# The causal mask of the forget-gate heads: subtracted from the decay by VectorE instead of multiplied in by TensorE

## The reference

```
def causal_block_attention(q, k, v, scale, log_decay=None):
    ...
        s = jnp.einsum('bhqd,bhkd->bhqk', qi, k, preferred_element_type=jnp.float32) * scale
        if log_decay is not None:
            s = s + args[2][..., :, None] - log_decay.astype(jnp.float32)[:, :, None, :]
        q_pos = i * Q_BLOCK + jnp.arange(Q_BLOCK)
        mask = key_pos[None, :] <= q_pos[:, None]
        s = jnp.where(mask, s, jnp.finfo(jnp.float32).min)
        p = jax.nn.softmax(s, axis=-1)
        return jnp.einsum('bhqk,bhkd->bhqd', p.astype(v.dtype), v)
    ...
    log_f = jax.nn.log_sigmoid(f_logit.astype(jnp.float32) + b_forget.astype(jnp.float32))
    c = jnp.cumsum(log_f, axis=1).transpose(0, 2, 1)
    o_fox = causal_block_attention(heads(fq), heads(fk), heads(fv), FOX_HEAD_DIM ** -0.5, c)
```

## Time and profile before

| | us |
|---|---|
| median of three runs (lowest, highest) | 2709.56 (2707.67, 2709.72) |
| span of the profiled execution, first to last instruction | 2705.4 |
| attention loop, 352.2 to 659.6 | 307.4 |
| first forget-gate half, 388.0 to 427.3 | 39.3 |
| first latent half after it, 427.3 to 464.5 | 37.2 |

### The profile page before, as it was taken

The page is one execution under the profiler, slowest core; times in us unless marked ns, Lnnn a source line. Parts: engine busy times, 40 slices in busy tenths (PEclk is TensorE's granted clock), DMA queues, the critical chain, the costliest instruction groups (busy, mean ns, idle before and its releaser), DMA issues.

```text
span 2705.4 us, 49571 instructions
## 1 busy us (share of the span) xinstructions
PE 2638.0 (98%) x17206; PEld 2118.7 (78%) x17207; DVE 1091.5 (40%) x2701; ACT 627.4 (23%) x1386; POOL 379.9 (14%) x391
## 2 busy tenths in 40 slices
PE   9999999999999998999999999999999999999997
PEld 8455556666477774999999999998878787878785
DVE  1111145554212324433333344344455454545455
ACT  0333355553011112011111111111212121221212
POOL 0100022221000001111111111111111111112111
PEclk9999999999999998999999999999999999999998
DMA  8111243232300002765667677787888888888885
GB/s 293 47 51 54 64 151 90 79 116 92 129 1 9 31 31 103 303 209 194 221 218 254 225 276 260 269 274 264 318 299 319 301 310 306 312 297 312 300 310 202
DMA packets 108856, 533.95 MB, mean 197 GB/s; under 512 B 24290, under 2 KB 59042, under 8 KB 84208
## 3 DMA queue, kind: packets, MB, share of 16 engines
q1 hardware_dynamic: 88016, 498.99, 50.2%
q0 software_dynamic: 20768, 33.97, 5.7%
HBM read 506.64 MB, written 60.52 MB: 210 GB/s over the span
## 4 chain that ended last, share of the span: by engine, by line
PE 92%; DVE 3%; issue 2%; DMA 2%; ACT 1%; DVEq 1%; POOL 0%; ACTq 0%; POOLq 0%
PE bank L1376 45%; PE wide L1376 9%; PE wide L1836 9%; PE wide L1804 9%; PE bank L1426 8%; PE bank L1369 4%; PE wide L1500 2%; PE bank L1556 2%; PE bank L1760 2%; PE wide L1517 1%; DMA d_sum<-y_sb,sidx 1%; PE wide L1369 1%; DVE biased L2060 1%; DVE prob_t L2071 1%; ACT prob L1151 0%
## 5 line engine op out<-in xcount | busy, mean ns | idle before, releaser
L1376 PE MATMUL bank<-xe_t,slot 128*128 128x128 f32 (+4 forms) x8192 | 1025.2, 287 | 12.3 <-issue 11.2
L1376 PEld LDWEIGHTS bank<-xe_t,slot 128*128 128x128 f32 x8192 | 1014.5, 192 | 14.1 <-issue 13.7
L2336 DVE TENSOR_SCALAR glu<-bank,b_gu 128x256 f32<-128x256 f32 x256 | 123.8, 484 | 657.2 <-PE bank L1376 657.1
L1317 ACT ACTIVATE sig<-glu 128x256 f32<-128x256 f32 x256 | 106.7, 417 | 837.8 <-DVE glu L2336 835.5
L1836 PE MATMUL wide<-slot,act_t 128*128 128x512 f32 x608 | 267.8, 593 | 1.0 <-DVE act_t L2348 1.0
L1804 PE MATMUL wide<-act_t,slot 128*128 128x144 f32 (+3 forms) x1664 | 235.5, 302 | 0.0
L1804 PEld LDWEIGHTS wide<-act_t,slot 128*128 128x128 f32 x1664 | 231.8, 190 | 0.0
L1426 PE MATMUL bank<-w_in,xt 128*128 128x512 f32 (+1 forms) x512 | 217.6, 575 | 1.6 <-DVEq L1978 1.6
L1836 PEld LDWEIGHTS wide<-slot,act_t 128*128 128x128 f32 x608 | 112.5, 190 | 128.8 <-issue 126.2
L1334 ACT ACTIVATE y_t<-wide,b_dn 128x256 f32<-128x256 f32 x248 | 102.0, 471 | 421.2 <-PE wide L1836 212.9
L955 POOL DMA_INDIRECT xg<-d_xn,gidx x66 | 66.6, 1009 | 862.8 <-DVE gidx L2290 814.0
(11 more groups left out here) (302 smaller groups left out, 2455.6 us busy)
## 6 DMA issues: line engine op xcount, KB each, us to landing
slot<-in_w_gu SPq DMA_DIRECT2D x128, 2048.0 KB, 8.8
slot<-in_w_dn SPq DMA_DIRECT2D x64, 2048.0 KB, 7.7
w_in<-in_w_in SPq DMA_DIRECT2D x1, 6144.0 KB, 25.3
w_mem_k<-in_w_mem_kv SPq DMA_DIRECT2D x4, 1024.0 KB, 11.0
w_mem_v<-in_w_mem_kv SPq DMA_DIRECT2D x1, 4096.0 KB, 20.6
x_sb<-in_x SPq DMA_DIRECT2D x8, 512.0 KB, 3.3
cneg<-d_cneg SPq DMA_DIRECT2D x8, 512.0 KB, 6.6
d_vw<-mix_out SPq DMA_DIRECT2D x16, 256.0 KB, 2.2
```

Of the source, the lines that this page charges most:

```text
L1317: ac.activation(sig[m % 2][:, :], glu[m % 2][:, :], ACT.Sigmoid, scale=1.702).then_inc(e_sig, 1)
L1376: m = pe.matmul(dst, l, r_, start=(k == 0), stop=(k == n - 1))
L2336: ve.tensor_scalar(glu[b][:, :], pp[b][:, 0:CAP], b_gu[:, bass.ds(e * 2 * KD + 2 * m, 1)], 7.0, ALU.add, ALU.min).then_inc(e_glu, 1)
```

## The change

The four mask matmuls per forget-gate tile go, and with them the swapped copies of identity and mask and their loads at the start. Instead VectorE subtracts the mask (0 or -1e30) from the block of the decay row that stands on the diagonal of the tile, in place, before `row_low` adds that row to the scores. A block so changed is spoilt for any longer tile, so the tiles must come in descending order; to keep long and short tiles in turn, there are two copies of the decay, one of full length for tiles 7, 6, 5, 4 and one of 512 columns (`cneg_short`) for tiles 3, 2, 1, 0. The order of the forget-gate tiles becomes 7, 3, 6, 2, 5, 1, 4, 0.

```
-        B_TILES = [6, 0, 7, 1, 5, 2, 4, 3]
-        B_PAIRS = [(y, i) for y in range(2) for i in B_TILES]
+        B_TILES = [[6, 0, 7, 1, 5, 2, 4, 3], [7, 3, 6, 2, 5, 1, 4, 0]]
+        B_PAIRS = [(y, i) for y in range(2) for i in B_TILES[y]]
...
             load(bf_row[:, :], a["b_forget"][0].partition_broadcast(P), ld["row_bias"])
             load(br_row[:, :], a["b_router"][0].partition_broadcast(P), ld["row_bias"])
-            for c in range(2):
-                for g in range(2):
-                    load(swapped[g * S.DN:(g + 1) * S.DN, c, :],
-                         a["const"][(1 - g) * S.DN:(2 - g) * S.DN, 2 * c * P:(2 * c + 1) * P], ld["swapped"])
...
                 for a_ in range(2):
                     load(cneg[a_][:, :], d_cneg[bass.ds(h * 2 + a_, 1), :].to_broadcast([P, T]), b_cneg.full)
+                    load(cneg_short[a_][:, :], d_cneg[bass.ds(h * 2 + a_, 1), 0:SHORT * P].to_broadcast([P, SHORT * P]),
+                         b_cneg.full)
...
-            po.wait_ge(ld["swapped"], 96)
-            po.tensor_copy(ident_x[:, :], swapped[:, 0, :]).then_inc(init, 1)
-            po.tensor_scalar(mask_x[:, :], swapped[:, 1, :], -1.0, None, ALU.mult).then_inc(init, 1)
...
                     for a_ in range(2):
-                        pe.matmul(wide[a_][:, c:c + w], q_fox[half[a_], i * P:(i + 1) * P], k_fox[half[a_], c:c + w],
-                                  start=True, stop=c + w < L)
-                for idn, tri_mask, stop in ((ident_b, mask_b, False), (ident_x, mask_x, True)):
-                    for a_ in range(2):
-                        m = pe.matmul(wide[a_][:, L - P:L], idn[half[a_], :], tri_mask[half[a_], :], start=False, stop=stop)
-                        if stop:
+                        m = pe.matmul(wide[a_][:, c:c + w], q_fox[half[a_], i * P:(i + 1) * P], k_fox[half[a_], c:c + w],
+                                      start=True, stop=True)
+                        if c + w == L:
                             m.then_inc(b_s[a_].full, 1)
...
                 n = y * NP + a_ * NT + i
+                if y == 1:
+                    decay = (cneg_short if i < SHORT else cneg)[a_]
+                    if p == NT and a_ == 0:
+                        ve.wait_ge(b_cneg.full, 64 * (h + 1))
+                        apart(ve)
+                    ve.tensor_tensor(decay[:, L - P:L], decay[:, L - P:L], mask, ALU.subtract)
+                    ve.drain()
                 ve.wait_ge(b_s[a_].full, NP * h + p + 1)
...
-                    if p == NT and a_ == 0:
-                        ve.wait_ge(b_cneg.full, 32 * (h + 1))
                     ve.wait_ge(b_p[a_], NP * h + p)
                     apart(ve)
-                    ve.tensor_tensor_reduce(biased[a_][:, 0:L], wide[a_][:, 0:L], cneg[a_][:, 0:L], 1.0, 3e38, ALU.add,
+                    ve.tensor_tensor_reduce(biased[a_][:, 0:L], wide[a_][:, 0:L], decay[:, 0:L], 1.0, 3e38, ALU.add,
                                             ALU.min, low[:, n:n + 1]).then_inc(b_s[a_].free, 1)
```

More of the change, by code:

```diff
@@ L131, in build @@
         w_r = keep("w_r", [P, KD, E])
-        ident_x, mask_x = (nc.alloc_sbuf_tensor_at(n, [P, P], BF16, offset=w_r_at + 2 * P * k)
-                           for k, n in enumerate(("ident_x", "mask_x")))
-        rn_t_at = keep.at
         rn_t = keep("rn_t", [P, KD, P])
@@ L158, in build @@
         mem_ss = r("mem_ss", [P, 4])
-        swapped = Region(127, 128)("swapped", [P, 2, P])
         r = Region(63, 95)
@@ L211, in build @@
         rr_row = [r(f"rr_row{y}", [2 * NT, P]) for y in range(2)]
+        SHORT = 4
+        assert base + 30 * 1024 <= a_end and keep_at >= w_r_at + 6 * 1024
+        cneg_short = [nc.alloc_sbuf_tensor_at(f"cneg_short{a_}", [P, SHORT * P], F32, offset=at_)
+                      for a_, at_ in enumerate((base + 28 * 1024, w_r_at + 4 * T))]
         r = Region(159, 167)
@@ L218, in build @@
         r = Region(191, 207)
-        cneg = [r("cneg0", [P, T]), nc.alloc_sbuf_tensor_at("cneg1", [P, T], F32, offset=rn_t_at)]
+        cneg = [r("cneg0", [P, T]), nc.alloc_sbuf_tensor_at("cneg1", [P, T], F32, offset=w_r_at)]
         rr_all = r("rr_all", [P, T])
@@ L351, in build @@
         NP = 2 * NT
-        B_TILES = [6, 0, 7, 1, 5, 2, 4, 3]
-        assert sorted(B_TILES) == list(range(NT))
-        B_PAIRS = [(y, i) for y in range(2) for i in B_TILES]
+        B_TILES = [[6, 0, 7, 1, 5, 2, 4, 3], [7, 3, 6, 2, 5, 1, 4, 0]]
+        assert all(sorted(x) == list(range(NT)) for x in B_TILES)
+        assert all(sorted(x, reverse=True) == x for x in ([i for i in B_TILES[1] if (i < SHORT) == u] for u in (False, True)))
+        B_PAIRS = [(y, i) for y in range(2) for i in B_TILES[y]]
         B_ROWS = (NT, NP - 1)
@@ L412, in build @@
             "small", "mem", "mem_1", "w_mem_v", "w_in", "rope", "w_o", "w_xq", "w_xo",
-            "w_r", "bias", "g_fin", "swapped", "last_heads")}
+            "w_r", "bias", "g_fin", "row_bias", "last_heads")}
         stage_end, passed = sem("stage_end"), sem("passed")
@@ L612, in _ @@
             load(w_mem_v[:, :, :], rows(a["w_mem_kv"][0])[:, :, D:2 * D], ld["w_mem_v"])
-            load(bf_row[:, :], a["b_forget"][0].partition_broadcast(P), ld["swapped"])
-            load(br_row[:, :], a["b_router"][0].partition_broadcast(P), ld["swapped"])
-            for c in range(2):
-                for g in range(2):
-                    load(swapped[g * S.DN:(g + 1) * S.DN, c, :],
-                         a["const"][(1 - g) * S.DN:(2 - g) * S.DN, 2 * c * P:(2 * c + 1) * P], ld["swapped"])
+            load(bf_row[:, :], a["b_forget"][0].partition_broadcast(P), ld["row_bias"])
+            load(br_row[:, :], a["b_router"][0].partition_broadcast(P), ld["row_bias"])
             w = rows(a["w_in"][0])
@@ L1474, in _ @@
             arrive(pe)
-            pe.wait_ge(init, 8)
+            pe.wait_ge(init, 6)
             pe.wait_ge(ld["w_in"], 80)
@@ L1967, in _ @@
             barrier(ve, 1)
-            ve.wait_ge(ld["swapped"], 96)
+            ve.wait_ge(ld["row_bias"], 32)
             ve.memset(rsum[:, :], 0.0)
```

## The result

The changed kernel takes 2721.5 us (median of 4 runs, 2720.7 to 2723.4) against 2708.6 for the kernel before (4 runs beside it): a ratio of 1.005, with an interval of 1.0038 to 1.0063. The forecast was 2721.6. In a second set of runs it was 2721.7 against 2707.7, ratio 1.0051 (1.0037 to 1.0065).

A forecast was written before the change was run, and what follows sets the result against it. TensorE, on 92% of the chain, was taken as the bound. Per half -1.66 + 3.63 + 1.3 = +3.3 us; four +13.1, less the last half's end +12.7, taken as +12 on 2709.56: 2721.6 us, range 2711 to 2731.

The forecast's parts named there:

- Masks: Forget-gate halves: dropping four bf16 matmuls per tile saves TensorE 1.66 us a half, 6.6 us over four.
- Order and VectorE's new work: Forget-gate halves: new tile order and subtractions raise TensorE's waits from 2.11 to 5.74 us, +3.63 a half.
- POOL: Forget-gate halves: POOL blocks tile 2's second-head subtraction, delaying tile 5's scores, +1.3 us a half (bounds 0 to 4.25).
- Latent halves: Latent-attention halves: unchanged but for the last tile's shorter values at their start; moving over 0.5 us would refute the forecast.
- The end of the last half: End of the last forget-gate half: TensorE's 0.42 us wait for the reciprocals is saved, as tile 0 finishes sooner.
- Loads and start at nothing: Program start and half ends: fewer start loads win nothing; two more loads per head pair cost nothing, being covered.
- (a): Rival, forget-gate halves: POOL costs nothing, its collisions falling in VectorE's waits; +7.5 us, 2717; chance 0.18.
- (b): Rival, forget-gate halves: faster, VectorE hides all added work, leaving only the 6.6 us of masks; 2703; chance 0.10.
- (d): Rival, forget-gate halves: waits grow only 1.7 us a half and cancel the removed masks; 2709; chance 0.10.
- (c): Rival, forget-gate halves: POOL costs more, two whole operations in each half's chain; +24.5 us, 2734; chance 0.12.

The follow-up runs named there:

- no-mask run: The kernel before without the four small mask matmuls of each forget-gate tile, order and loads unchanged; loop 303.85 us against 307.38.
- no-subtraction run: The changed kernel without VectorE's mask subtractions, new order and extra decay loads kept; loop 306.11 us against 321.60.
- no-POOL run: The changed kernel without POOL's three operations normalising the latent half's output in each forget-gate half; loop 315.21 us against 321.60.
- order-alone: The kernel before with only the new order of forget-gate tiles, masks still on TensorE; 2710.0 us against 2707.2, ratio 1.0008.

## Why the prediction was right, and where its terms were not

The mechanism is shown: TensorE's work stays, the added subtractions stand between the two heads' minima, TensorE waits at the banks behind them, and POOL stretches one of them in each half (a second, briefly, where tile 5 is hit). Taking the subtractions away returns the whole loss, and placing them elsewhere returns 13 us of it. Taken one after the other, the four parts come, in the loop, to -3.5 (masks, no-mask run), +2.3 (order and loads, no-subtraction run less no-mask run), +9.1 (subtractions without POOL, 315.21 - 306.11) and +6.4 (POOL, 321.60 - 315.21). Each is the difference of two neighbouring runs, so that they add up to the measured +14.2 by construction; the bank waits of the first half bear out the last two. The predicted sum of +12 hit the median because its errors offset each other: the mechanism was right, but that it came within 0.1 us is luck.

- **Masks, -6.6 predicted, -3.5 measured.** The step that failed is the reading of 0.21 us from the first mask to the next instruction as all gain: 0.10 of it passes without masks too. Start to start of the same two f32 groups in both cases would be the right measure.
- **Order and VectorE's new work, +14.5 predicted, +11.4 measured.** The single waits of the first half against the prediction: 0.71 for 0.82, 1.44 for 1.75, 0.47 for 0.77, 0.34 for 0.56, 0.35 for 0.41, 1.04 for 1.43; the places are right and each is too long. One cause shows: the gap behind a subtraction is 0.26 us, not 0.30, so the second head was late by 0.37 instead of 0.41. That does not account for all of it.
- **POOL, +1.3 a half predicted.** The place (second head of tile 2, scores of tile 5) and the size (1.36) came out in the profiled first half; 1.08 and 0.86 in two others. In one half of each profile the collision fell on tile 5 instead and the clock fell after it. The prediction had the collisions after tile 2's at 0.2 us or less and hidden, and nothing on the clock. That makes the term +6.4 instead of +5.2.
- **Latent halves.** The prediction let them be unchanged but for the shorter values of the last tile, which are 0.65 us in each of three halves. They got that work off, and the first two did not get shorter: 37.33 and 37.29 against 37.25 and 37.24. TensorE instead waits for ScalarE there (`ACT prob_t`), 0.77 us in place of 0.17 in the first of these. The latent halves are together 0.26 us shorter instead of 1.95, a loss of 1.7 us that the sum did not have. The first forget-gate half adds up with it: -0.89 (masks) + 2.24 (bank waits) + 1.36 (POOL) + 0.65 (values) = 3.36 of the 3.74 measured; most of the rest, 0.32, is again in the start-to-start times of the transposes.
- **The end of the last half, -0.4.** Right: the wait of 0.42 us for the reciprocals is gone, and the products of the row sums (674.66) follow those before them without a wait.
- **Loads and start at nothing.** Nothing speaks against it: the no-subtraction run has the new loads and the shorter start, a loop shorter than before's, and a loop that starts at 352.10 us against 352.23.
- **The rivals.** (a) is excluded by the no-POOL run, (b) and (d) by the result. But (b) states what the change could have been: with both heads' work ahead of the wait it is level with before, and with no subtractions at all only 1.3 us ahead. (c) did not come in the change itself; with doubled subtractions POOL stretched three in a row.

Open: what the clock needs to fall behind a wait, and why the first of the forget-gate halves is 0.2 to 0.5 us longer than the next two in some versions.

## What to carry to other kernels

When work moves to an engine that has spare time, look at which side of that engine's waits it lands: the same 64 operations cost 15.5 us between two heads' minima and 2.2 us ahead of the wait for scores. Price removed instructions by start-to-start times of the instructions on both sides that stay, since part of the time may pass without them too (here 0.10 of 0.21 us). And ask first for the ceiling: here a run without the new work at all was only 1.3 us faster in the loop, less than this kernel's measurement can tell.

## What was not expected of the hardware

Behind a wait of TensorE of 1.9 us the granted clock was at 1.2 GHz for 3.4 us, in a loop in which it otherwise stands at 2.4; a collision that made one subtraction 1.5 us longer so cost its half 3.1 to 3.2 us against the run without POOL. At the start of the program, from 12 to 16 us, the granted clock was 0.57 in the first profile of the changed kernel and 1.00 in the second; the order-alone and no-POOL profiles read 0.57 and 0.58, that of before 1.00. This differs between runs of one kernel. With it goes a later start of the loop: 353.93 to 354.12 us in the three profiles with 0.57 or 0.58, 352.10 to 352.88 in the other nine. It is not charged to the change.
